# A two-layer transformer kernel on one core: x loaded by token tile ahead of the weights, two steps moved up in VectorE's order, and feed-forward splits made three chunks ahead

## The reference

```python
h = rms_norm(x, norm_mix_pre[l])
proj = h @ w_in[l]                       # q, kv, gates, dq, dkv, conv input, pool input
o_a = compressed + selected + windowed attention   # keys compressed in blocks of 32 by an MLP
o_b = conformer_conv(b_in, ...)          # 31 taps, layer norm, silu
o_c = pool_mixer(c_in, ...)
o_d = banded_attention(qd, kd, vd, 128, sinks)
gates = sigmoid(h @ w_gate[l])           # 4 branches x 1024
mix = sum_n(gates_n * (o_n @ w_branch[l, n])) @ w_o[l]
x = x + rms_norm(mix, norm_mix_post[l])
hf = rms_norm(x, norm_ffn_pre[l])
u = causal_depthwise_conv(hf @ ffn_w_up[l], ...)   # width 3, 2 x 2816 channels
x = x + rms_norm((gelu(gate) * val) @ ffn_w_down[l], norm_ffn_post[l])
```

## Time and profile before

| | us |
|---|---|
| median of 3 runs | 1973.1 |
| lowest and highest of them | 1967.58, 1974.57 |
| profiled execution, its own time | 1964.29 |
| its span | 1962.5 |
| mean granted TensorE clock in it | 0.942 of full speed |

### The profile page before, as it was taken

One profiled execution on the slowest core, in us unless ns is written; L12 is line 12 of the kernel. 1 busy time (PEld: TensorE's weight loads), 2 busy tenths in 40 slices (PEclk: granted clock), 3 DMA queues, 4 the chain that ended last, 5 costly groups with the idle time before them and its releaser, 6 DMA issues. The chain is left out here.

```text
span 1962.5 us, 26709 instructions
## 1 busy us (share of the span) xinstructions
PE 1780.0 (91%) x10780; PEld 1450.0 (74%) x10780; DVE 1072.9 (55%) x1474; ACT 749.5 (38%) x1041; POOL 378.5 (19%) x333
## 2 busy tenths in 40 slices
PE   5898899899998898999899998999899896899996
PEld 4687679788986786679788984545476546799995
DVE  3657766654745567776645731164554416354555
ACT  3443456444634353455444621123224302334341
POOL 0212222223511222212124501013320001000000
PEclk9999999899999899999899999899969997799998
DMA  5453445445554454425455554221100042255552
GB/s 214 150 194 129 153 148 179 165 174 213 197 204 151 150 184 152 158 108 198 144 207 205 185 191 158 84 86 65 43 22 1 1 150 73 103 190 176 188 181 75
DMA packets 39961, 282.02 MB, mean 144 GB/s; under 512 B 4784, under 2 KB 5040, under 8 KB 6704
## 3 DMA queue, kind: packets, MB, share of 16 engines
q1 hardware_dynamic: 37984, 272.44, 38.1%
q10 hardware_dynamic: 1872, 8.08, 1.2%
HBM read 279.45 MB, written 1.05 MB: 143 GB/s over the span
## 5 line engine op out<-in xcount | busy, mean ns | idle before, releaser
L420 DVE TENSOR_TENSOR ring_low<-ring,sb_hi 128x2048 fp32r<-128x2048 f32 (+1 forms) x116 | 240.9, 2077 | 316.9 <-ACT sb_hi L413 316.8
L413 ACT ACTIVATE sb_hi<-ring 128x2048 fp32r<-128x2048 f32 x116 | 222.3, 1916 | 276.8 <-DMA ring<-weights 137.3
L572 PE MATMUL psum<-sb_hS,sb_hi 128*128 128x256 f32 x704 | 205.0, 291 | 20.9 <-DVE sb_rkT L1185 15.3
L818 PE MATMUL psum<-sb_hfT,ring_low 128*128 128x256 f32 x704 | 202.7, 288 | 0.0
L575 PE MATMUL psum<-sb_hS,sb_hi 128*128 128x256 f32 x704 | 201.4, 286 | 0.0
L576 PE MATMUL psum<-sb_hS,ring_low 128*128 128x256 f32 x704 | 200.8, 285 | 0.0
L1807 DVE TENSOR_TENSOR sb_split<-ring,sb_split 128x2048 fp32r<-128x2048 f32 x48 | 110.0, 2292 | 160.3 <-ACT sb_split L1802 160.3
L572 PEld LDWEIGHTS psum<-sb_hS,sb_hi 128*128 128x128 f32 x704 | 136.0, 193 | 32.5 <-DVE ring_low L420 21.5
L2100 PE MATMUL psum<-sb_hfS,sb_split 128*128 128x256 f32 x512 | 146.4, 286 | 2.5 <-PE psum L2122 2.1
L420 POOL TENSOR_TENSOR ring_low<-ring,sb_hi 128x1024 fp32r<-128x1024 f32 x28 | 92.7, 3309 | 287.4 <-ACT sb_hi L413 287.4
L2103 PE MATMUL psum<-sb_hfS,sb_split 128*128 128x256 f32 x512 | 145.9, 285 | 0.0
(11 more groups left out here) (382 smaller groups left out, 4229.0 us busy)
## 6 DMA issues: line engine op xcount, KB each, us to landing
ring<-weights SPq DMA_DIRECT2D x256, 1024.0 KB, 4.8
sb_rows_ffn<-rows ACTq DMA_DIRECT2D x4, 512.0 KB, 5.7
sb_rows_mix<-rows ACTq DMA_DIRECT2D x2, 1024.0 KB, 5.0
sb_rows<-rows ACTq DMA_DIRECT2D x1, 2048.0 KB, 9.1
sb_cols<-cols ACTq DMA_DIRECT2D x2, 686.0 KB, 7.9
sb_x<-x_in SPq DMA_DIRECT2D x1, 1024.0 KB, 4.9
sb_y<-ctx_in SPq DMA_DIRECT2D x1, 1024.0 KB, 6.1
out<-sb_x SPq DMA_DIRECT2D x2, 512.0 KB, 2.6
```

Source lines behind the costliest of these rows:

```text
L413: act.activation(hi_of(n), ring[:, c % SLOTS, :], ACT.Copy).then_inc(hi_ready, 1)
L420: eng.tensor_tensor(low_of(n)[:, half], ring[:, SPLIT_CHUNKS[n] % SLOTS, half], hi_of(n)[:, half].bitcast(F32), ALU.subtract)\
L572: mm = pe.matmul(out, hi[:, k, bs], hS[:, 0, k, :], start=(k == 0), stop=False)
L818: mm = pe.matmul(out, lo[:, k, b * P:(b + 1) * P], hfT[:, 0, k, :], start=False, stop=(k == KD - 1))
```

## The change

- x is loaded in two halves with a semaphore for each token tile; `const` is laid out so that the identity and `mhalf` (the exponent of the root) come first and are loaded with a semaphore of their own (`turner_in`); only chunk 0 follows them in the first block. Chunks 1 to 3, the rest of the constants, the columns and the sinks are issued by SP in the second block.
- The pre_mix row is issued by ScalarE at the start of the first block. In layer 0 ScalarE splits chunk 0 after it has scaled tile 0, and chunk 1 after the high parts of the transposed tiles; VectorE's low parts stand at the matching places, and it waits for the rest of the constants after them.
- The copies of the rotated keys move ahead of the low part of the second chunk of `FIRST_BA`.
- `cmp_mask` and `cmp_weigh` move ahead of the ten convolution steps of turn 1.
- In the feed-forward loop both halves of a chunk are made three chunks ahead (`AHEAD = 3`); the number of places stays four.

```diff
+AHEAD = 3
 CONST, N_CONST = offsets([
-    ("ident", P), ("tri_u", P), ("tri_l", P), ...
+    ("ident", P), ("mhalf", 32), ("tri_u", P), ("tri_l", P), ...
+TURNER = CONST["mhalf"][0] + CONST["mhalf"][1]
...
-        pe.wait_ge(placed, 16)
+        pe.wait_ge(turner_in, 16)
         turn_normed("ht", 1)
...
         squares_of(0)
         norm_first(0)
+        if l == 0:
+            split_hi(act, 0)
...
         high_parts("ht", hS)
+        if l == 0:
+            split_hi(act, 1)
...
         high_parts("hf", hfT)
-        for n in range(FIRST_FFN + 2, FIRST_FFN + 4):
-            split_hi(act, n)
+        split_hi(act, FIRST_FFN + 2)
...
-                split_hi(act, FIRST_FFN + j + HI_FFN)
-        for n in range(FIRST_DOWN + HI_FFN, len(SPLIT_CHUNKS)):
+                split_hi(act, FIRST_FFN + j + AHEAD)
+        for n in range(FIRST_DOWN + AHEAD, len(SPLIT_CHUNKS)):
...
         gains(0)
         norm_second(0)
+        if l == 0:
+            split_lo(dve, 0)
         low_parts("ht", 0, hS)
+        if l == 0:
+            split_lo(dve, 1)
+            dve.wait_ge(placed, 16)
...
-        for i in range(2):
-            split_lo(dve, FIRST_BA + i)
+        split_lo(dve, FIRST_BA)
         for t in range(TT):
             jobs.wait_filled(dve, ("rkT", t))
             jobs.drain(dve.tensor_copy(rkT[...], jobs.out(("rkT", t))[...]), ("rkT", t))
+        split_lo(dve, FIRST_BA + 1)
...
-            conv_steps(10)
             if i == 1:
                 cmp_mask()
                 cmp_weigh()
+            conv_steps(10)
...
         low_parts("hf", 1, hfT)
-        for n in range(FIRST_FFN + 2, FIRST_FFN + 4):
-            split_lo(dve, n)
+        split_lo(dve, FIRST_FFN + 2)
...
-            split_lo(dve, FIRST_FFN + j + HI_FFN)
+            split_lo(dve, FIRST_FFN + j + AHEAD)
...
-        for n in range(FIRST_DOWN + HI_FFN, len(SPLIT_CHUNKS)):
+        for n in range(FIRST_DOWN + AHEAD, len(SPLIT_CHUNKS)):
...
-        pool.wait_ge(placed, 16)
+        pool.wait_ge(turner_in, 16)
         pre_roots(0)
...
                 @block.sync          # first block
                     sp.dma_start(mem["cond"][:, :], cond).then_inc(conditioned, 16)
-                    sp.dma_start(mem["x"][:, :, :], x_in.rearrange("(t p) d -> p t d", p=P)).then_inc(loaded, 16)
-                    sp.dma_start(mem["const"][:, :], const).then_inc(placed, 16)
-                    for s in range(SLOTS):
-                        sp.dma_start(ring[:, s, :], weights[s]).then_inc(landed[s], 16)
+                    for t in range(TT):
+                        sp.dma_start(mem["x"][:, t, :], x_in[t * P:(t + 1) * P, :]).then_inc(loaded[t], 16)
+                    sp.dma_start(mem["const"][:, 0:TURNER], const[:, 0:TURNER]).then_inc(turner_in, 16)
+                    sp.dma_start(ring[:, 0, :], weights[0]).then_inc(landed[0], 16)
                 @block.scalar        # first block
+                    layers[0]["heads"]["load_pre"](act)
                     act.wait_ge(conditioned, 16)
...
                 @block.sync          # second block
+                    for s in range(1, SLOTS):
+                        sp.dma_start(ring[:, s, :], weights[s]).then_inc(landed[s], 16)
+                    sp.dma_start(mem["const"][:, TURNER:], const[:, TURNER:]).then_inc(placed, 16)
+                    layers[0]["heads"]["load_cols"](sp)
                 @block.scalar        # second block
-                    layers[0]["heads"]["load_pre"](act)
-                    layers[0]["heads"]["load_cols"](act)
-                    layers[0]["heads"]["highs"](act)
                 @block.vector        # second block
-                        if layer is layers[0]:
-                            layer["heads"]["lows"](dve)
```

More of the change, by code:

```diff
@@ L75 @@
 CONST, N_CONST = offsets([
-    ("ident", P), ("tri_u", P), ("tri_l", P), ("ones", P), ("full_causal", 2 * P), ("band", 2 * P),
+    ("ident", P), ("mhalf", 32), ("tri_u", P), ("tri_l", P), ("ones", P), ("full_causal", 2 * P), ("band", 2 * P),
     ("cmp_mask", 32), ("cmp_valid", 2), ("blk8", 8), ("rope", 192), ("axial", 192),
-    ("pool_inv", 64), ("mhalf", 32), ("four", 4), ("sel", 32),
+    ("pool_inv", 64), ("four", 4), ("sel", 32),
 ])
+TURNER = CONST["mhalf"][0] + CONST["mhalf"][1]
 def constants():
@@ L283, with layer_block @@
 BRANCH_ORDER = (2, 0, 3, 1)
-def layer_block(nc, l, mem, ring, ring_low, landed, used, wts, psum, sems, cols_dram, rows_dram, placed, wait_x, wait_scratch):
+def layer_block(nc, l, mem, ring, ring_low, landed, used, wts, psum, sems, cols_dram, rows_dram, turner_in, placed, wait_x, wait_scratch):
     filled = {r: sems(f"filled_{r}") for r in REGION}
@@ L2806, in build_program @@
         used = [ctx.enter_context(nc.semaphore(f"used_{s}")) for s in range(SLOTS)]
-        loaded = ctx.enter_context(nc.semaphore("loaded"))
+        loaded = [ctx.enter_context(nc.semaphore(f"loaded_{t}")) for t in range(TT)]
+        turner_in = ctx.enter_context(nc.semaphore("turner_in"))
         placed = ctx.enter_context(nc.semaphore("placed"))
@@ L2831, in build_program, with sems, wait_x, wait_scratch @@
             place(first, MEM_FFN)
+            layer_sems = []
+            def sems(name):
+                s = first.enter_context(nc.semaphore(name))
+                layer_sems.append(s)
+                return s
+            layers = []
+            for l in range(LAYERS):
+                def wait_x(eng, t, before=layers[-1]["x_ready"] if l else None):
+                    if before is None:
+                        eng.wait_ge(loaded[t], 16)
+                    else:
+                        eng.wait_ge(before, TT + t + 1)
+                def wait_scratch(eng, before=layers[-1]["post_sq"] if l else None):
+                    if before is not None:
+                        eng.wait_ge(before, 4 * TT)
+                layers.append(layer_block(nc, l, mem1, ring, ring_low, landed, used, weights, psum,
+                                          lambda name, l=l: sems(f"{name}_{l}"), cols, rows, turner_in, placed, wait_x, wait_scratch))
+            heads = [layer["heads"] for layer in layers[1:]] + [None]
             with nc.Block() as block:
@@ L2857, in _ @@
                     pool.wait_ge(zeroed, 5)
-            layer_sems = []
-            def sems(name):
-                s = first.enter_context(nc.semaphore(name))
-                layer_sems.append(s)
-                return s
-            layers = []
-            for l in range(LAYERS):
-                def wait_x(eng, t, before=layers[-1]["x_ready"] if l else None):
-                    if before is None:
-                        eng.wait_ge(loaded, 16)
-                    else:
-                        eng.wait_ge(before, TT + t + 1)
-                def wait_scratch(eng, before=layers[-1]["post_sq"] if l else None):
-                    if before is not None:
-                        eng.wait_ge(before, 4 * TT)
-                layers.append(layer_block(nc, l, mem1, ring, ring_low, landed, used, weights, psum,
-                                          lambda name, l=l: sems(f"{name}_{l}"), cols, rows, placed, wait_x, wait_scratch))
-            heads = [layer["heads"] for layer in layers[1:]] + [None]
             with nc.Block() as block:
```

## The result

The changed kernel takes 1899.6 us (median of four executions, 1897.5 to 1965.4) against 1972.3 us for the kernel before on the same chip: a ratio of 0.963, 95% interval 0.961 to 0.966. Forecast were 1902 us. The profiled execution took 1900.4 us, its span fell from 1962.5 to 1898.4 us: 64.1 us, where the sum said 70.6. Each experiment has its ratio to executions of the kernel before beside its own; their median was 1971.7, 1969.3 or 1968.9 us (1972.3 beside the kernel after). So times of two runs that lie a few us apart are to be compared by their ratios.

A forecast was written before the change was run, and what follows sets the result against it. TensorE, busy for 91% of the span, bounds the kernel; only its idle or low-clock time can be won. 9.5 + 23.3 + 10.4 + 27.4 = 70.6 us off 1964.3 gives 1893.7; plus 8.8 for the median, 1902 us, range 1888 to 1928.

The forecast's parts named there:

- the sum: Whole kernel: the four parts' gains add to 70.6 us off the profiled execution's 1964.3 us, giving 1893.7 us.
- The head: Start of the kernel: first projection starts at 15.75 in place of 26.30; 9.5 us won, between 7.5 and 11.
- Key copies: Ahead of the second low split, both layers: TensorE's wait and its low clock go; 23.3 us won.
- Compressed softmax: Ahead of ten convolution steps: 4.0 us of wait and 1.2 us of clock a layer; 10.4 us won.
- Three ahead: Feed-forward loops: all six modulation-row waits go, 14.3 us, plus 13.1 us of low clock; 27.4 us won.
- 1.0 us for the clock: Head: loss from TensorE's 1.2 us pause before the first projection, middle of 0 and 2.2 us.
- a pause of 1.5 us is nearer to the 1.87 us that left the clock alone: Before part bg 0: the remaining pause leaves the clock up, so 1.7 us lost after 114.51 are won too.
- The slack against starvation: Feed-forward loop: with a lead of three, 1.5 us to spare before TensorE needs a chunk's low part.
- 1: Rival, whole kernel: idle time comes back but the clock doesn't; 47 us won, 1926 us; chance 0.13.
- 2: Rival, feed-forward loops: stalls stay because ScalarE is late for another reason; 43 us won, 1930 us; chance 0.12.
- 3: Rival: copies are held by something the view doesn't name, only the head is won; 10 us, 1963 us; chance 0.03.
- 4: Rival, feed-forward loops: a lead of three is too short, low parts come late; slower, 1983 us; chance 0.03.

The follow-up runs named there:

- rk_back: The changed kernel with the key copies put back behind the second low split of the part; 1919.5 us, ratio to before 0.977.
- head_back: The kernel before with the other three parts (key copies, compressed softmax, three ahead) and its old head; 1911.1 us, ratio to before 0.971.
- cmp_back: The changed kernel with mask and weighing of the compressed softmax put back behind the ten convolution steps; 1910.5 us, ratio to before 0.970.
- ahead4: The changed kernel with the feed-forward lead put back from three chunks to four; 1927.9 us, ratio to before 0.978.
- weigh_first: The changed kernel with gate chunk 7's low split moved from the end of attention turn 4 behind turn 5's weighing; 1891.8 us, ratio to before 0.962.
- weigh_warm: The changed kernel with both the low split moved behind turn 5's weighing and unneeded matmuls filling TensorE's idle stretches; 1888.6 us, ratio to before 0.960.
- turn_later: The changed kernel with a feed-forward lead of four and each modulation row turned one part later; 1903.5 us, ratio to before 0.965.
- ahead2: The changed kernel with a feed-forward lead of two chunks in place of three; 1903.6 us, ratio to before 0.967.
- warm: The changed kernel with matmuls nobody reads put in TensorE's idle time around the norms' transposes; 1894.7 us, ratio to before 0.963.

## Why the prediction was right, point by point

The total held (1899.6 against 1902), and all four mechanisms are shown, each by a run that puts its part back. That the total is so close is in part luck. The sum gave 1893.7 us for a profiled execution, and the profiled one took 1900.4: 6.7 us more. The forecast then added 8.8 us, because the median before lay so far above its profiled execution, and that didn't carry over: the median after lies 0.8 us below its own. The two misses come near to cancelling. The profiled execution before was one of the best of its kernel, at a mean clock of 0.942. Of 20 more executions beside the experiments 3 took 1964.2 to 1964.5 us with 0.941 or 0.942, and 17 took 1966.6 to 1974.1 us with 0.936 to 0.940.

To price the parts I take from each mark what the falls of turn 5 cost this execution, by the granted clock of the 12 us behind the pause (0.72, 3.4 us a fall; in rk_back 0.57, 5.2 us), for they come and go in the same code:

| | mark | falls in turn 5 | mark without them | worth of the part | forecast |
|---|---|---|---|---|---|
| before | 1131.7 | 0 | 1131.7 | | |
| after | 1068.1 | 2 | 1061.4 | all: 70.4 | 70.6 |
| head_back | 1072.1 | 1 | 1068.7 | head 7.4 | 9.5 |
| rk_back | 1086.3 | 1 | 1081.1 | key copies 19.7 | 23.3 |
| cmp_back | 1074.7 | 0 | 1074.7 | softmax 13.4 | 10.4 |
| ahead4 | 1091.4 | 1 | 1088.0 | three ahead 26.7 | 27.4 |

The four add up to 67.2 us, near the 70.4 of the whole. The correction is worked out, not measured; without it they are 4.0, 18.2, 6.6 and 23.3. It leaves in the slow start of the head: the kernel after has it, head_back and rk_back don't, so by an estimate these two parts are worth some 2 us more than the table says. With one profiled execution each, differences of 2 to 3 us between worth and forecast can't be explained from these runs.

- **The head (9.5 us, 7.4 in the table).** The start was right to 0.4 us, by two errors that half cancel: x later (6.63 for 5.5; the price of a DMA that the prediction cites would have had it at 4.4), the way through the roots shorter. "1.0 us for the clock" stands for both ends of its range (0 and 2.2), and both occur: the kernel after lost 1.9 us (the first refill of the ring that SP issues behind the first projection came at 24.05, 7.9 us after the first matmul, where before it took 6.0, 26.30 to 32.31), and runs with the same head lost next to nothing. Counted at the gates' transposes (74.05 before) the head was worth 7.9 us in the kernel after and 9.5 to 10.2 us in the four quick ones (64.55 to 63.89).
- **Key copies (23.3, 19.7 in the table).** From the gates' transposes to bg 0 it is 30.4 us now and was 40.5 before, so bg 0 started 10.1 us sooner than the head alone explains (10.3 forecast). The step that failed is "a pause of 1.5 us is nearer to the 1.87 us that left the clock alone": the pause was 1.89 in layer 0, with the clock at 1.00, but 2.19 in layer 1, with 0.79. Nor is there a length that divides the two: at this place the clock fell after 1.80 us (weigh_first, layer 1: 0.79) and stayed at 1.00 after 2.35 us (weigh_warm, layer 0).
- **Compressed softmax (10.4, 13.4 in the table).** The wait went as worked out, leaving pauses of 0.46 us. The clock behind it was undervalued: cmp_back shows 0.69 over 8 us, of which TensorE was busy for 7.00, so 2.2 to 2.5 us, where 1.2 was taken.
- **Three ahead (27.4).** Both loops went from 150.2 to 136.0 us, 28.5 together; ahead4 and turn_later show that it is the copy's wait and its clock and nothing else. The slack against starvation was misjudged, as ahead2 shows, without bearing on the sum; in the kernel after no wait on ring_low stands in the loops.
- **What the sum left out (6.7 us).** That a pause which the change doesn't touch can begin to cost. It took the earlier trace rows's 1.00 after 1.87 us in turn 5 as a property of the place. It is not: over the profiled executions of all kernels that have this pause (twelve, two layers each) the clock fell in 11 of 24, after pauses of 1.56 to 1.77 us, and stayed in 13, after 1.48 to 1.87 us. What decides is not shown; I count it as a chance. The kernel after had both falls, which is 6.7 us, as much as the 6.5 by which the span missed.
- **The rivals.** 1 (idle time alone, 1926 us) falls: with ahead4, 15.6 us of wait cost 26.7. 2 and 3 fall by the rows of waits. 4 falls by ahead2.

The Trainium skill (TensorE: Matmul & The Clock Gate, section HAM oscillation) describes how a wait inside a loop lets TensorE fall back to the low clock, each time anew, with wall time lost beyond the wait. The rows of ahead4, rk_back and cmp_back agree: 15.6, 15.3 and 9.4 us of wait cost 26.7, 19.7 and 13.4 by the table.

## What to carry to other kernels

Where an engine works through a fixed order, look for the instruction that waits for a transfer and ask what stands behind it that another engine wants sooner: four such moves of a few lines (one of them of the head's whole order) were worth 3.7%, and a fifth that the wait view had shown all along (5.9 us on sb_sc) was left. Price a wait of TensorE of some us at 1.3 to 1.7 times its length, for the clock after it; a short pause counts as a chance, so don't read "no loss" from one execution. When parts are priced one by one, compare at a mark directly behind the changed code, for the same code behind it varied by 7.5 us here; and before a difference is put down to an edit, look whether other runs with the same code show it too (the start of the head varied by 2 us under one code).

## What the runs showed of the hardware

- Pauses of 1.5 to 1.9 us at the same instruction (turn 5) dropped the granted clock in 11 of 24 cases and left it in 13; the length doesn't order them. ahead4, turn_later and ahead2 ran the same instructions as the kernel after up to this pause in layer 0, and all four fell (0.58 to 0.64); in layer 1 two of the four did.
- Matmuls on zeros raise the clock as real ones do: in warm, 7.04 us of them ahead of the head's transposes brought these from 3.65 to 1.91 us. Matmuls on constants did the same ahead of the feed-forward part (3.67 to 2.13 us).
- In the head of the kernel after the matmuls ran 0.43 us apart until 20.13 while the granted clock's row says 1.00; only the count of matmuls in a window (26 against 36) shows it. Three of the seven runs with this head show it, four don't. At the start of these traces the row of the clock can't be taken at its word.
- 32 KB of conditioning took 3.5 us to land while the row and x were on their way (1.9 us before), and a tile of x, half of it, took 5.9 us (median of the two), against 4.9 us for all of x before.
